# A hybrid decoder step: the feed-forward's last part by token chunks, and attention steps for two heads at once

## The reference, cut to what matters

```python
def stick_breaking(q, k, v, q_pos, k_pos, bias):
    z = einsum('bqhd,bkhd->bhqk', q, k) * DH_A ** -0.5 + bias
    mask = k_pos[None, :] < q_pos[:, None]
    log_beta = log_sigmoid(z)
    log_keep = where(mask, log_sigmoid(-z), 0.0)
    later = cumsum(log_keep, axis=3, reverse=True) - log_keep
    att = where(mask, exp(log_beta + later), 0.0)
    return einsum('bhqk,bkhd->bqhd', att, v)

# around each mixer f, and around swiglu, in each layer:
x = x + rms_norm(f(rms_norm(x, g_pre)), g_post)
# swiglu
(silu(h @ w_gate) * (h @ w_up)) @ w_down
```

## Time and profile before

| what | us |
|---|---|
| median of 3 runs | 3670.26 |
| lowest, highest | 3657.05, 3670.46 |
| the profiled execution, its own time | 3668.21 |
| its span, first to last instruction | 3666.4 |
| PE, DVE, ACT, POOL busy in it | 3434.1, 1819.7, 1217.9, 410.6 |
| mean granted TensorE clock (1.0 is 2.4 GHz) | 0.962 |

### The profile page before, as it was taken

How to read it: one execution, slowest core, us unless ns; L and a number is a source line. 1 busy time by engine, 2 the same in 40 slices (tenths; PEclk the granted TensorE clock), 3 DMA queues, 4 the chain that set the end, 5 groups by cost and what they waited for, 6 DMA issues and landing times. The chain is left out here.

```text
span 3666.4 us, 53174 instructions
## 1 busy us (share of the span) xinstructions
PE 3434.1 (94%) x19948; PEld 3101.8 (85%) x19948; DVE 1819.7 (50%) x3368; ACT 1217.9 (33%) x2254; POOL 410.6 (11%) x876
## 2 busy tenths in 40 slices
PE   7999788999999899999999979988889999999997
PEld 7999675666566599999999978987569999999996
DVE  6444316565666675344334465324667434334436
ACT  5433234544454563111111144112446211211113
POOL 0000213323233040000000000000205000000000
PEclk9999889999899999999999989998989999999998
DMA  5332553222111151111111111223533111111111
GB/s 142 99 102 98 167 156 87 67 53 76 33 38 29 58 154 47 46 40 46 40 46 40 46 30 60 90 71 134 172 95 104 52 40 40 51 40 40 40 52 49
DMA packets 346747, 263.18 MB, mean 72 GB/s; under 512 B 79045, under 2 KB 309769, under 8 KB 346596
## 3 DMA queue, kind: packets, MB, share of 16 engines
q1 hardware_dynamic: 334776, 218.34, 20.4%
q0 software_dynamic: 11824, 42.93, 3.2%
HBM read 202.60 MB, written 58.62 MB: 71 GB/s over the span
## 5 line engine op out<-in xcount | busy, mean ns | idle before, releaser
L449 PE MATMUL ffn_ps<-heads_hi,ffn_w_hi 128*128 128x368 f32 x2496 | 829.7, 332 | 14.3 <-DVE ffn_w_lo L923 14.3
L450 PE MATMUL ffn_ps<-heads_lo,ffn_w_hi 128*128 128x368 f32 x2496 | 828.0, 332 | 0.0
L451 PE MATMUL ffn_ps<-heads_hi,ffn_w_lo 128*128 128x368 f32 x2496 | 824.5, 330 | 0.0
L449 PEld LDWEIGHTS ffn_ps<-heads_hi,ffn_w_hi 128*128 128x128 f32 x2496 | 471.6, 189 | 16.7 <-DVE ffn_w_lo L923 15.2
L450 PEld LDWEIGHTS ffn_ps<-heads_lo,ffn_w_hi 128*128 128x128 f32 x2496 | 470.6, 189 | 1.6 <-issue 0.3
L451 PEld LDWEIGHTS ffn_ps<-heads_hi,ffn_w_lo 128*128 128x128 f32 x2496 | 471.5, 189 | 0.0
L449 PE MATMUL ffn_ps<-ffn_h_hi,ffn_w_hi 128*128 128x368 f32 x1056 | 349.7, 331 | 0.0
L451 PE MATMUL ffn_ps<-ffn_h_hi,ffn_w_lo 128*128 128x368 f32 x1056 | 349.0, 331 | 0.0
L450 PE MATMUL ffn_ps<-ffn_h_lo,ffn_w_hi 128*128 128x368 f32 x1056 | 348.2, 330 | 0.0
L1030 DVE TENSOR_TENSOR mix<-ffn_ps,mix 128x368 f32<-128x368 f32 x480 | 255.3, 541 | 170.8 <-PE ffn_ps L451 170.1
L449 PE MATMUL ab_ps<-pre_hi,ab_w_hi 128*128 128x368 f32 x624 | 220.0, 353 | 9.2 <-DVE pre_lo L311 7.7
(11 more groups left out here) (498 smaller groups left out, 6262.0 us busy)
## 6 DMA issues: line engine op xcount, KB each, us to landing
out_w_first<-in_w_ffn_gate_dram SPq DMA_DIRECT2D x44, 512.0 KB, 3.8
ffn_w_raw<-in_w_ffn_up_dram SPq DMA_DIRECT2D x44, 512.0 KB, 3.9
first_w_raw<-in_w_in_ab_dram SPq DMA_DIRECT2D x27, 512.0 KB, 4.1
out_w_first<-in_w_ffn_down_dram SPq DMA_DIRECT2D x22, 512.0 KB, 4.5
ffn_w_raw<-in_w_ffn_down_dram SPq DMA_DIRECT2D x22, 512.0 KB, 3.6
rwkv_prep<-xT POOLq DMA_DIRECT2D x4, 2208.0 KB, 7.4
qkv_proj<-qk_out_sb POOLq DMA_DIRECT2D x16, 552.0 KB, 3.0
atts_k_page<-in_cache_k_dram SPq DMA_DIRECT2D x32, 256.0 KB, 2.9
```

The lines of the kernel that those rows point to most:

```text
L449: pe.matmul(out, w_hi, x_hi, start=first, stop=False)
L450: pe.matmul(out, w_hi, x_lo, start=False, stop=False)
L451: return pe.matmul(out, w_lo, x_hi, start=False, stop=last)
```

## The change

Five things are done together.

- In the last of the 11 parts, gate, up and down of the second hidden tile go chunk by chunk: gate, up and eight down outputs of chunk 0, then of chunk 1, then of chunk 2. A down output's half for hidden tile 0 is computed first for k = 0 to 3, then the halves for tile 1.
- Squares of the result are added on POOL. PE sums chunk 0's squares inside the gate matmuls of chunk 1 and so on; ACT and DVE make that chunk's norm factor between silu and h, with a table load for Ln and Exp in each; norm, residual, high and low parts of finished elements are put among the down outputs of chunks 1 and 2. 12 of 24 elements are done so in layer 0, 16 in layer 1 (without high and low).
- `project_qkv` begins with element 12, sums chunk 0's squares at once, adds the squares of chunks 1 and 2 on POOL so that one matmul is enough for each, has its first weight tile loaded in the stage before, and its second unit waits for each chunk's copy alone. `store_added` begins with element 16.
- Attention steps take both heads of a pair and blocks of 256 queries: 100 steps for 120, with the same columns in all. ACT scales each head by itself (another bias); all other ACT and DVE operations of a step take both heads in one instruction. Scores are one matmul for each head; sums and rest are one for both; values are one for each head, into the partitions 0 to 63 and 64 to 127 of one bank.
- Keys are loaded by halves of their columns for both heads, values with both heads' 128 features in a row.

The core of the diff (of the two `last_part`, ACT's stands first, then DVE's):

```diff
+                if ch * KT + k >= self.begin:
+                    pool.wait_ge(self.sq_done, ch * KT + k + 1 - self.begin)
+                pool.tensor_tensor(at, at, self.y[:, k, chunk(ch)], ALU.add).then_inc(self.sq_added, 1)
...
     def sum_on_tensor(self, pe, ch):
         if ch:
             pe.wait_ge(self.log_done, ch)
+            pe.wait_ge(self.sq_added, (KT - 1) * ch)
+            mm = pe.matmul(self.bank, self.c["ones"][:, :], self.y[:, 0, chunk(ch)], start=True, stop=True)
...
-            for p in range(2):
-                sp.wait_ge(lo_done[p], 1)
-                load(0, p)
+            sp.wait_ge(ahead.loaded, 16)
+            sp.sem_inc(raw_in[0], 16)
+            sp.wait_ge(lo_done[1], 1)
+            load(0, 1)
...
+            x.sum_on_tensor(pe, 0)
+            for ch in range(2):
+                for p in range(2):
+                    for k in range(KT):
+                        first_unit(p, ch, k)
+            for k in range(KT):
+                if k == 2:
+                    x.sum_on_tensor(pe, 1)
+                for p in range(2):
+                    first_unit(p, 2, k)
+            x.sum_on_tensor(pe, 2)
...
+            def last_part():
+                for ch in range(NCH):
+                    if ch == 2:
+                        element(at)
+                        at += 1
+                    silu(LAST, 1, [ch])
+                    if ch:
+                        load_exp_ln(nc, act)
+                        tail_root(ch - 1)
+                        for _ in range(ch):
+                            element(at)
+                            at += 1
+                    split_h(LAST, 1, [ch])
+                    if ch == 2:
+                        element(at)
+                        at += 1
+                    for k in range(KT):
+                        down_square(ch * KT + k)
+                        if ch and k in (2, 5):
+                            element(at)
+                            at += 1
...
+            def last_part():
+                for ch in range(NCH):
+                    if ch == 2:
+                        for _ in range(2):
+                            element(at)
+                            at += 1
+                    if ch:
+                        weigh(ch - 1)
+                    scale(LAST, 1, False, [ch])
+                    if ch:
+                        tail_rstd(ch - 1)
+                        for _ in range(2):
+                            element(at)
+                            at += 1
+                    mult(LAST, 1, ch)
+                    split_h(LAST, 1, ch)
+                    for k in range(KT):
+                        down_add(ch * KT + k)
+                        if ch and k in (1, 4, 7) and at < UNITS_OUT + KT * ch:
+                            element(at)
+                            at += 1
...
+                for k in range(KT):
+                    mm = three_passes(pe, ps[:, 3 * (m % 2) + ch, 0:CW], w_hi[:, m % RING, k, :], w_lo[:, m % RING, k, :],
+                                      hi[:, k, chunk(ch)], lo[:, k, chunk(ch)], k == 0, k == KT - 1)
+                    if m == 2 and ch and k == 6:
+                        sum_y(NCH + ch - 1)
...
+                for k in range(4):
+                    half(k, 0)
+                pe.wait_ge(h_lo_done, LAST * UNITS + (NCH + ch + 1 + 3))
+                for k in range(4):
+                    half(k, 1).then_inc(down_mm, 1)
+                for k in range(4, KT):
+                    half(k, 0)
+                    half(k, 1).then_inc(down_mm, 1)
...
-    G = 512
+    G = 256
...
+                for hh in range(2):
+                    mm = pe.matmul(att[0:keys, Z, hh, lo:width], k_in[:, hh, k0:k0 + keys],
+                                   q_in[:, i % 2, q0 + lo:q0 + width], start=True, stop=not diag, skip_group_check=True)
...
-                pe.matmul(att[0:keys, LOG, lo:width], neg_tri[0:keys, 0:keys], keep_hi[0:keys, n % 2, lo:width],
+                pe.matmul(att[0:keys, LOG, :, lo:width], neg_tri[0:keys, 0:keys], keep_hi[0:keys, n % 2, :, lo:width],
...
-                pe.matmul(att[pair(hh), O, lo:width], v_in[0:keys, kt, hh, :],
-                          w[0:keys, n % 2, lo:width], start=first[n], stop=last, skip_group_check=True
-                          ).then_inc(pv_mm, 1)
+                for hh in range(2):
+                    mm = pe.matmul(att[pair(hh), O, 0, lo:width], v_in[0:keys, kt, hh, :],
+                                   w[0:keys, n % 2, hh, lo:width], start=first[n], stop=last, skip_group_check=True)
+                mm.then_inc(pv_mm, 1)
...
+                        for hh in range(2):
+                            head = 2 * steps[t][0] + hh
+                            act.activation(zs[0:keys, t % 3, hh, lo:width], att[0:keys, Z, hh, lo:width], ACT.Identity,
+                                           scale=DH ** -0.5, bias=bias8[0:keys, head:head + 1]).then_inc(z_scaled, 1)
...
-                        dve.tensor_copy(mix[pair(hh), i, q0:q0 + width], att[pair(hh), O, 0:width]).then_inc(out_done, 1)
+                        dve.tensor_copy(mix[:, i, q0:q0 + width], att[:, O, 0, 0:width]).then_inc(out_done, 1)
```

More of the change, by code:

```diff
@@ L403, in on_act @@
             between(n)
-            if n == 2 * KT + 4:
+            if ch * KT + k == 2 * KT + 1:
                 root(0)
-        for n in range(KT * NCH - LAG, KT * NCH):
+        for n in range(len(self.order) - LAG, len(self.order)):
             square(n)
@@ L425, in on_dve @@
         LAG = 3
-        for n in range(KT * NCH + LAG):
-            if n < KT * NCH:
+        for n in range(len(self.order) + LAG):
+            if n < len(self.order):
                 ch, k = self.order[n]
@@ L778, in _ @@
                     add_x_square(e)
+            for n in range(UNITS_OUT, 2 * UNITS_OUT):
+                if n % KT:
+                    add_y_square(n)
         @block.scalar
@@ L837, in first_split, with silu @@
                 split(0, m)
-            def silu(i, t):
-                for ch in range(NCH):
+            def silu(i, t, chunks=range(NCH)):
+                for ch in chunks:
                     u = i * UNITS + (t * NCH + ch)
@@ L850, in split_h, with one @@
                     act.activation(h_hi[:, t, chunk(ch)], h[:, ch, :], ACT.Copy).then_inc(h_hi_done, 1)
-            def squares():
-                for d in range(DOWN):
-                    k, ch = d // NCH, d % NCH
-                    act.wait_ge(down_added, (F_PARTS - 1) * DOWN + (d + 3))
-                    if k >= 3:
-                        act.wait_ge(sums.added, d - 3 * NCH + 1)
-                    to = ysum[:, chunk(ch)] if k == 0 else (gate if k % 2 else h)[:, ch, :]
-                    act.activation(to, mix[:, k, chunk(ch)], ACT.Square).then_inc(sums.squared, 1)
-            def one(i, last):
+            def one(i):
                 silu(i, 0)
@@ L868, in one, with down_square, tail_root, element @@
                 split_h(i, 1)
-                if not last:
-                    for m in range(3):
-                        split(i + 1, m)
+                for m in range(3):
+                    split(i + 1, m)
+            def down_square(d):
+                k, at = place(d)
+                n = UNITS_OUT + d
+                act.wait_ge(down_added, LAST * DOWN + (d + 3))
+                square_free(n)
+                act.activation(square_at(n), mix[:, k, at], ACT.Square).then_inc(y_squared, 1)
+            def tail_root(ch):
+                t = h[:, ch, :]
+                act.wait_ge(t_weighed, 2 * ch + 2)
+                act.activation(t, t, ACT.Ln, bias=eps[:, 0:1], scale=1.0 / D_MODEL).then_inc(t_log, 1)
+                act.wait_ge(t_log, ch + 1)
+                act.activation(t, t, ACT.Exp, scale=-0.5).then_inc(t_root, 1)
+            def element(e):
+                if pre2 is not None and e < ELEMENTS:
+                    x_high_and_square(e)
+            def last_part():
+                silu(LAST, 0)
+                split(LAST, 3)
+                split_h(LAST, 0)
+                split(LAST, 4)
+                split(LAST, 5, RING)
+                act.wait_ge(w_lo_done[5], ROUNDS + F_PARTS)
+                at = UNITS_OUT
+                for ch in range(NCH):
[18 more added lines that the diff above has]
+                            at += 1
+                while at < ELEMENTS:
+                    element(at)
+                    at += 1
+                tail_root(2)
             heads_high(0)
@@ L1000, in _, with down_add @@
             dve.sem_inc(down_added, 2)
[L1002 to L1010 removed]
+            def down_add(d):
+                k, at = place(d)
+                dve.wait_ge(down_mm, LAST * DOWN + (d + 2))
+                dve.tensor_tensor(mix[:, k, at], ps[:, LAST_BANK[d], 0:CW], mix[:, k, at], ALU.add).then_inc(down_added, 1)
@@ L1011, in one @@
+            def one(i, first):
                 scale(i, 0, first)
@@ L1018, in one @@
                 for k in range(KT):
```

(6 more changed lines are left out.)

464 lines of the change are left out of this document (279 added, 185 removed).

## The result

| | median us | lowest, highest | runs |
|---|---|---|---|
| before | 3667.97 | 3657.05, 3677.26 | 20 |
| after | 3652.45 | 3642.82, 3662.31 | 20 |

The ratio is 0.9967, with an interval of 0.9959 to 0.9976: the change saves 12 us by the ratio and 15.5 by the medians, where 39 to 41 were forecast. That is faster, but within 0.5%, the case that had 0.19. The time lies inside the forecast's range of 3603 to 3664, which says little for the mechanism: less than half of the gain came, and the attention stage is 735.2 us long, where the prediction named 725 or more as a sign that it was wrong. Runs of one kernel lie up to 11 us from their median.

What follows compares the result with a forecast made beforehand. PE's work, plus what the recurrence's chain leaves uncovered, was taken to bound the attention stage. Savings of 28 (attention), 9.5 (layer 0) and 3.8 (layer 1) made 41 us, forecasting 3629 us, range 3603 to 3664.

Steps and rivals of the forecast that it cites:

- the case that had 0.19: Whole kernel: the time after stays within about 0.5% (18 us) of before, chance 0.19.
- 725 or more as a sign that it was wrong: Attention stage: expected near 707 us; 725 or more would make the prediction wrong.
- The prices of the attention's matmuls: Attention: values of both heads cost one head's 0.58 us, 39.5 saved; sums and rest 7.6 saved; scores 1 lost.
- the rival in which they don't: Attention values: the two heads' halves run one after another; total 7 us saved, 3663; chance 0.08.
- 46 less work: Attention stage: PE's work falls by 39.5 + 7.6 - 1 = 46 us.
- I let 40% of the gain turn into such waits and take 28 us: Attention stage: part of the 46 us becomes PE waits at the recurrence's hops; 28 saved, between 18 lost and 47.
- slower: the clock in the attention stage: Attention stage: thinner work lowers the granted clock c, stage takes 645/c; 3690 us at 0.84; chance 0.05.
- the recurrence's chain takes the gain: Attention stage: PE finishes earlier but waits for ACT's and DVE's copies; attention saves 8, total 21, 3649 us; chance 0.18.
- Layer 0's handovers: Layer 0, last feed-forward part: PE waits for sums of squares and for h, 2x(1.3+3.1)+1.3 = 10.1 us lost.
- From the last down matmul to the second unit: Layer 0: stage end 9.0 us plus `project_qkv` 41.5; with the handovers 60.6 against 70.1, 9.5 saved.
- the 4.0 that I added for DVE beside POOL: `project_qkv`: DVE slowed beside POOL's 14 adds, 4.0 us added; 9 if DVE lost 1 us at each.
- The store: End of layer 1: 20.8 us from the barrier to the span's end, 34.2 now; layer 1 in all 3.8 saved.

Runs made afterwards that it cites:

- `old_steps_lean`: The kernel before, with the low-part matmuls left out of sums and rest (216 fewer): 3651.09 us, ratio 0.9949 to before.
- `new_steps_twice`: The kernel before with the change's attention steps alone, each values product issued twice: 3674.62 us, ratio 1.0020 to before.
- `attn_only`: The kernel before with only the attention steps of the change, on the old feed-forward: 3655.94 us, ratio 0.9968 to before.
- `handover_first`: The changed kernel with next chunk's h ahead of the chunk's norm on ACT and DVE, squares summed inside up: 3641.84 us, ratio 0.9928 to before.
- `new_hop_weights`: The change's attention steps alone on the kernel before, plan weights 2 for x, sa, y, s: 3634.99 us, ratio 0.9922 to before.

## Why the prediction was right and wrong

**The prices of the attention's matmuls held.** Values 0.58, as in the sum; the halves run together, and the rival in which they don't is out. Counted at full clock the stage went from 691 to 651 us, 40 less where 46 less work was forecast, with 16 us more of waits in it. The Trainium skill's TensorEngine Tiling (Array Packing), Instruction Overhead, gives each matmul an overhead of about 60 cycles, which speaks against smaller ones; it is not borne out here: four records of 256 columns for two heads take what two of 256 for one head did.

**The step that failed** is "I let 40% of the gain turn into such waits and take 28 us". Measured are 12 us by medians, 7 in the profiles. Two things were wrong in it. The share was a guess that no row carried: `old_steps_lean` and `new_steps_twice` show that a little under half reaches the end with an unchanged plan, not 60%. And what took the rest was called waits, where most of it is seen in the clock, which the sum put at nothing in this stage: against before, `attn_only` loses 33 us more to the clock in the profiles, 27 over all executions, and has 16 us more of waits (the two overlap). The rival "slower: the clock in the attention stage" had the right form: 645/0.89 is 725, and the stage took 730. I gave it 0.05 because only below 0.86 does it make the kernel slower. But at 0.94 the 645 us would take 686 and at 0.89 they take 725: of these 39 my sum covered the 18 that I had let go as waits. I wrote against that rival that "dense pieces are nearly all PE". They are, in part at 1.2 GHz. The time fell next to the rival "the recurrence's chain takes the gain" (3649), but not for its reason, so that rival's number is luck: lengthening the hops by 21 us cost the new steps no more than the old ones.

**What turned the gain into lost clock is the plan.** With its weights as they were and 100 steps of less work, the waits at the hops grew from 12.4 to 20.4 us. With the hops' weights at 2 the attention change alone brings 28.4 us, and the stage's clock is 0.92. That this is the size of the term that I had forecast is chance: my sum had the old plan and no clock in it. That the plan decides is shown by the same edit on both kinds of steps (17 to 21 us on the new ones, none on the old). That the time goes with the clock is seen over all executions; that the low clock makes it longer, and isn't only its companion, and which of the pauses lets the clock fall, is argued from timelines only. Filling PE's pauses with other matmuls, which would part the clock from the waits, wasn't tried.

**Layer 0's handovers** were forecast at 10.1 us and cost 15.0. The waits were not the error: 3.4 us for two sums (forecast 2.6) and 4.2 for two parts of h (forecast 6.2). The term was short of the clock again: 0.92 over 63 us is 5.0 us more, and with the two sums' own 1.3 us this makes 13.9 of the 15.0. Before, PE is busy throughout this part at a clock of 1.00. The second sum and what follows it, in a timeline of PE in after:

```profile
2162.89 1.59 PE L1243 MATMUL ffn_ps<-ffn_gate,ones 128*128 128x368 f32 x2 [2.96 <-POOL ffn_gate L816]
2163.73 1.05 PE L463 MATMUL ffn_ps<-parts_hi,ffn_w_hi 128*128 128x368 f32 x1
2164.59 0.51 PE L464 MATMUL ffn_ps<-parts_lo,ffn_w_hi 128*128 128x368 f32 x1
2164.89 0.51 PE L465 MATMUL ffn_ps<-parts_hi,ffn_w_lo 128*128 128x368 f32 x1
```

Matmuls that start 0.168 us apart at 2.4 GHz start 0.30 apart here, at 1.2 GHz. In layer 1 it is 10.7 for 8.1: 6.9 us of waits and 2 of clock. `handover_first` shows that most of this wasn't needed: with the order alone 16 of these 26 us go away, and the kernel is 10.6 us shorter by the medians.

**From the last down matmul to the second unit** 50.5 us were forecast and 50.2 came out, with two errors that cancel:

```profile
2182.89 0.33 PE L465 MATMUL ffn_ps<-ffn_h_hi,ffn_w_lo 128*128 128x368 f32 x1
...
2188.99 1.59 PE L1243 MATMUL ffn_ps<-ffn_gate,ones 128*128 128x368 f32 x2 [5.77 <-POOL ffn_gate L816]
...
2194.35 2.18 PE L457 MATMUL qk_sum_ps<-mix,ones 128*128 128x368 f32 x3 [3.77 <-PEq L66]
...
2227.74 0.86 PE L454 MATMUL qk_sum_ps<-mix,ones 128*128 128x368 f32 x2 [0.71 <-POOL mix L392]
...
2233.07 0.64 PE L463 MATMUL qk_ps<-parts_hi,qk_w_hi 128*128 128x368 f32 x1 [3.86 <-DVE qk_out_sb L581]
```

The end took 11.5 us, forecast 9.0: POOL's last add was done 5.9 us after the last down matmul rather than 4.8, and from the sum to the barrier there were 5.4 us rather than 4.2, both beside a DVE that was at elements. `project_qkv` took 38.7, forecast 41.5: PE waits once, 0.71 us for POOL, and the 4.0 that I added for DVE beside POOL was too much. That DVE is slowed is seen in a timeline of POOL and DVE in after:

```profile
2182.22 2.60 POOL L816 TENSOR_TENSOR ffn_gate<-ffn_gate,ffn_w_raw 128x368 f32<-128x368 f32 x2 [0.31 <-ACT ffn_w_raw L929]
...
2182.69 1.31 DVE L1033 SCALAR_TENSOR_TENSOR mix<-mix,gains,rstd 128x368 f32<-128x368 f32 x1
...
2204.67 0.59 DVE L442 SCALAR_TENSOR_TENSOR mix<-mix,gains,rstd 128x368 f32<-128x368 f32 x1
```

The same form takes 1.31 us beside an add and 0.59 beside none, and two adds take 2.60 where one alone takes 1.00. By the rule of the Trainium skill's SBUF — State Buffer, Who interferes with whom, on the port pair shared by GpSimd and DVE, the second blocks wholly; the trace agrees, with 1.31 for 0.59. The 9 us in place of 4.0 that I worked out from it for the 14 adds didn't come, since DVE had time to spare there.

**The store.** From the last down matmul to the first transpose 12.7 us (forecast 9.0), from there to the end of the span 21.1 (forecast 20.8). In after, in order of time:

```profile
3626.51 0.33 PE L465 MATMUL ffn_ps<-ffn_h_hi,ffn_w_lo 128*128 128x368 f32 x1
...
3631.44 1.59 PE L1243 MATMUL ffn_ps<-ffn_gate,ones 128*128 128x368 f32 x2 [4.59 <-POOL ffn_gate L816]
...
3635.59 0.54 DVE L1042 TENSOR_TENSOR xT<-xT,mix 128x368 f32<-128x368 f32 x1
3636.05 0.53 DVE L1116 TENSOR_TENSOR ffn_h<-ffn_ps,rstd 128x368 f32<-128x368 f32 x1
...
3637.19 0.60 ACT L934 ACTIVATE ffn_h<-ffn_h,ffn_eps 128x368 f32<-128x368 f32 x1 [7.64 <-DVE ffn_h L1118]
...
3639.24 6.71 PE L1412 MATMUL store_ps<-ident,xT 128*128 128x128 f32 x40 [6.20 <-PEq L66]
```

PE's sum begins 4.9 us after the last down matmul, as forecast (4.8), but DVE takes up the norm only at 3636.05, 4.6 us later, because eight instructions of elements stand ahead of it in its queue: a queue that I had counted as "beside it". So layer 1 comes out 2.6 us slower, where 3.8 saved were forecast, and with layer 0 (5.1 saved for 9.5) the seams give 2.5 us in the profiles, where 13.3 were forecast, and nothing that the medians show.

## What to carry to other kernels

Where two streams of work are woven by a fixed plan, a leaner stream needs its plan balanced again: here the same matmuls in another order were worth 21 to 24 us, where the whole change brought 12 to 15.5. When PE's work shrinks beside a chain of hops, forecast the stage as (work at full clock) / (granted clock), and let the clock fall rather than assume it constant: a few short pauses close together can cost more by the slower matmuls behind them than by their own length (1.9 us of pauses from 1046.8 on stand ahead of some 20 us at 1.2 GHz in after). And when a norm is moved under matmuls, put the next matmul's operands first in every queue, and the norm behind them.

## What the hardware showed that was not expected

- The clock falls with little waiting. In after 0.92 over 63 us of which PE paused 7.5, and 0.73 over a piece of 50 us in which it was busy 44.6. Between `attn_only` and `new_hop_weights`, whose PE waits differ by 3.9 us in a stage of 700, the granted clock differs by 0.03, or 21 us.
- More matmuls can cost half of their length: the values issued twice put about 38 us of PE work into the stage, and the kernel is 19 us longer, while over all executions its clock rose from 0.955 to 0.960, 17 us less lost.
- Four fp32 records of 256 columns, two for each half of the output partitions, take 0.58 us, as one half's two did: the two halves cost no more than one.
